# Hybrid encoder layer on eight cores: one halo neighbour per core, first keys from unnormalised x, initial loads in order, halo and memory later

## The reference, cut to what matters

```python
h = rmsnorm(x, norm_gain); proj = h @ w_in          # x: 4 sequences of 4096 rows, D = 2048
q_a,k_a,v_a,z_a, u_b,v_b,z_b, q_c,z_c, gates = split(proj)
# A: |t-s| <= 128 attention, 12 heads over 4 key/value heads of 128, ALiBi, one sink logit
scores = q.k/sqrt(128) - slope*|t-s|;  outside the window or the sequence: -inf
o_a = softmax([scores, sink])[..., :-1] @ v * silu(z_a)
# B: gMLP in chunks of 128 rows: gelu(u) * (w_s[g] @ layernorm(gelu(v)) + b_s[g]) * silu(z_b)
# C: 4 heads of 256 over 256 memory rows: k,v = rmsnorm(mem, mem_norm_gain) @ w_kv_mem
merged = sum over branches of (o @ w_br) * sigmoid(gate)
out = rmsnorm(x + merged @ w_out, final_gain)
```

## Time and profile before

| | us |
|---|---|
| median of 3 runs | 2816.52 |
| lowest, highest | 2794.78, 3295.66 |
| the profiled execution's own time | 2794.82 |
| its span, slowest core (all 8: 2790.7 to 2793.3) | 2793.3 |
| PE busy | 2720.9 |
| DVE, ACT, POOL busy | 869.9, 623.8, 200.6 |

### The profile page before, as it was taken

The page is one execution under the profiler, slowest core; times in us unless marked ns, Lnnn a source line. Parts: engine busy times, 40 slices in busy tenths (PEclk is TensorE's granted clock), DMA queues, the critical chain, the costliest instruction groups (busy, mean ns, idle before and its releaser), DMA issues.

```text
span 2793.3 us, 34510 instructions; the slowest of 8 cores (2790.7 to 2793.3 us)
## 1 busy us (share of the span) xinstructions
PE 2720.9 (97%) x12953; PEld 1280.9 (46%) x13213; DVE 869.9 (31%) x1209; ACT 623.8 (22%) x1183; POOL 200.6 (7%) x381
## 2 busy tenths in 40 slices
PE   5899999999999999999999999999999999999996
PEld 2444456544444444444444444554444444444443
DVE  5600036570641112222450000767063222122224
ACT  3211134434111111111121112543411111111112
POOL 0000000000000000000000000000000000000000
PEclk8999999999999999999999999999999999999998
DMA  9254444624545555444997444222454444444484
GB/s 243 68 91 76 77 82 76 98 53 67 93 84 106 106 106 84 76 76 77 256 221 142 78 77 70 46 46 46 72 88 69 76 76 75 81 78 77 81 196 137
DMA packets 76003, 267.19 MB, mean 96 GB/s; under 512 B 8512, under 2 KB 8640, under 8 KB 74560
## 3 DMA queue, kind: packets, MB, share of 16 engines
q0 software_dynamic: 54288, 197.55, 43.1%
q1 hardware_dynamic: 21552, 67.41, 7.8%
HBM read 445.68 MB, written 16.78 MB: 166 GB/s over the span
## 4 chain that ended last, share of the span: by engine, by line
PE 95%; DVE 3%; issue 1%; ACT 1%; DMA 0%; DVEq 0%; ACTq 0%; SPq 0%
PE ps L333 88%; PE ps L711 2%; PE ps L675 1%; PE ps L678 1%; DVE hT L474 1%; DVE AR L457 1%; PE ps L445 1%; PE ps L772 0%; PE ps L812 0%; DVE OT L1092 0%; PE ps L919 0%; DVE AR L472 0%; DVE AR L474 0%; DMA OT<-xs 0%; DVE GN L726 0%
## 5 line engine op out<-in xcount | busy, mean ns | idle before, releaser
L333 PE MATMUL ps<-hT,RG 128*128 128x512 bf16 x7252 | 1658.7, 380 | 24.0 <-DVE hT L474 12.9
L333 PEld LDWEIGHTS ps<-hT,RG 128*128 128x128 bf16 x7424 | 725.1, 98 | 861.2 <-issue 33.6
L333 PE MATMUL ps<-OT,RG 128*128 128x512 bf16 x2009 | 456.1, 379 | 2.1
L283 POOL DMA_DIRECT2D RG<-wall x376 | 199.9, 532 | 2516.9 <-PE ps L333 1929.1
L726 DVE RECIPROCAL GN<-GN 128x256 f32<-128x256 f32 x96 | 161.5, 1724 | 584.5 <-ACT GN L722 584.5
L958 ACT ACTIVATE GN<-ps 128x512 f32<-128x512 f32 x192 | 113.7, 596 | 882.4 <-PE ps L333 882.4
L333 PEld LDWEIGHTS ps<-OT,RG 128*128 128x128 bf16 x2048 | 200.2, 98 | 240.7
L966 DVE TENSOR_TENSOR GN<-ps,GN 128x512 f32<-128x512 f32 x128 | 88.6, 692 | 550.0 <-PE ps L333 521.5
L333 PE MATMUL ps<-RG,AR 128*128 128x512 bf16 x1050 | 230.7, 379 | 1.2
L333 PE MATMUL ps<-RG,hT 128*128 128x512 bf16 x990 | 221.7, 379 | 1.2
L333 PEld LDWEIGHTS ps<-RG,AR 128*128 128x128 bf16 x1072 | 104.9, 98 | 126.5
(11 more groups left out here) (113 smaller groups left out, 1109.1 us busy)
## 6 DMA issues: line engine op xcount, KB each, us to landing
RG<-wall POOLq DMA_DIRECT2D x376, 512.0 KB, 6.2
OT<-xr SPq DMA_DIRECT2D x16, 1024.0 KB, 17.4
y<-OT SPq DMA_DIRECT2D x32, 512.0 KB, 4.0
OT<-xs SPq DMA_DIRECT2D x8, 1024.0 KB, 19.7
HX<-xr SPq DMA_DIRECT2D x16, 512.0 KB, 6.9
OT<-xt SPq DMA_DIRECT2D x16, 512.0 KB, 20.5
OT<-xh SPq DMA_DIRECT2D x4, 768.0 KB, 16.9
OT<-mt SPq DMA_DIRECT2D x4, 512.0 KB, 8.5
```

Source lines behind the costliest of these rows:

```text
L283: S.op("pool", lambda h: h.dma_start(out=RG[:, sl, :], in_=wall[row * 128:(row + 1) * 128, :]), r=list(gate), w=["R%d" % sl], dma=True)
L333: ins = h.matmul(psb(b, n), lhsT=pairs[i][0], rhs=pairs[i][1], start=(i == 0), stop=(i == N - 1))
```

## The change: what it does

1. **Mirror.** The second half of each sequence is laid out back to front (its rows reversed, the spatial weights and biases reversed with them, and the output turned back). Every core then has the sequence's end on its left and its one neighbour on its right. Block 0 is gone: halo is two blocks (9, 17), 256 rows, and tile 0's first score pack is 256 wide, not 384.
2. **Raw keys.** Slab 0 and slab 1 of x are multiplied by the gain alone into bf16 (`raw_piece`: ACT the first 1 or 2 of four `kc`, DVE the rest), and the key matmuls read that. The factor is applied when the keys leave PSUM (`k_scaled`, DVE). Values and all else still read the normalised `hT`, whose scaling now comes after the first keys.
3. **Loads in order.** x slab 0; key chunk 0 once the third of its four pieces has landed, chunks 1 to 3 behind it; x slab 1 once chunk 2 has landed; chunks 4 to 7 once the third piece of slab 1 has landed.
4. **Halo and memory later.** Their loads follow the first values; sums and scaling are spread over the z stage (`prep`); halo keys and values are computed after it (`kv_halo`), for which the 8 key and value chunks are loaded a second time.
5. Squares are first folded by DVE from four to two (L467), reciprocals come in halves, a table load is taken early, and dummy matmuls (`warm`) stand ahead of and between the first sums. Value evacuations are all ACT's.

```diff
     def tile(first):
         ...
+        if first:
+            p += [("k", g) for g in range(4)] + [("v", 0, q) for q in range(4)]
         for h in range(12):
...
-        HTH_OFF = 20480
-        hTh = view("AR", HTH_OFF, 6144, BF16).rearrange("p (k t) -> p k t", t=384)
+        HTH_OFF = 16384
+        hTh = view("AR", HTH_OFF, 4096, BF16).rearrange("p (k t) -> p k t", t=256)
...
         nS0.load()
-        load_chunk(0)
-        nS1.load()
-        for n in range(1, NSLOT):
-            load_chunk(n, gate=nS0.xc(15))
+        load_chunk(0, gate=nS0.xc(8))
+        for n in range(1, 4):
+            load_chunk(n)
+        nS1.load(gate=["R2"])
+        load_chunk(4, gate=nS1.xc(8))
+        for n in range(5, NSLOT):
+            load_chunk(n)
...
+        warm(48)
+        for p in range(4):
+            nS0.raw_piece(p, 1)
+            nS0.square(p)
+            nS0.fold(p, True)
+            if p < 3:
+                warm(8)
+        nS0.rstd()
...
+        def kv_first():
+            ks = [Ck(0, ("k", g)) for g in range(4)]
...
+            for g in range(4):
+                run(group(kraw(g), 512, "all", k_scaled(g, 1, nS0)))
+            nS0.scale(0, 10)
+            k1 = []
+            for p in range(4):
+                nS1.raw_piece(p, 2)
+                nS1.square(p)
+                nS1.fold(p, False)
+                if p == 0:
+                    k1 = [group(kraw(g), 512, "all", k_scaled(g, 5, nS1)) for g in range(4)]
+                for g in range(4):
+                    if p < 3:
+                        k1[g][p]()
...
+            for g in range(4):
+                k1[g][3]()
...
+            nS0.scale(10, 16)
+            v0 = [v_group(0, v, lb) for lb in range(1, 5)]
+            for q in range(4):
+                for t in range(3):
+                    v0[t][q]()
+                if q == 0:
+                    nS1.total()
+                    nS1.rstd()
+                    for a in hold:
+                        S.op(*a)
+                    nS1.scale()
+            run(v0[3])
+            v1 = [v_group(0, v, lb, sub=1) for lb in range(5, 9)]
+            for kc in range(16):
+                for t in range(4):
+                    v1[t][kc]()
+            v.free()
+            nH.load()
+            nM.load()
...
+                    if tt == 0:
+                        prep({4: 1, 6: 2, 8: 3, 10: 4}.get(ch0 + i, 0))
+            if tt == 0:
+                kv_halo()
```

More of the change, by code:

```diff
@@ new lines, in total, with rstd @@
+            def total(self):
+                w = self.w
+                self.b = bank()
+                S.op("pe", lambda h: h.matmul(psb(self.b, w), lhsT=ONEF[:], rhs=self.ac, start=True, stop=True),
+                     r=["onef"] + self.acc, w=pc(self.b))
+            def rstd(self):
+                w, rs = self.w, self.rs
+                S.op("act", lambda h: h.activation(out=rs, in_=psb(self.b, w), func=AF.Sqrt, scale=1.0 / D,
+                                                   bias=smc(c_eps)), r=["eps"], w=self.rsc + pc(self.b))
+                hw = w // 2
+                for q in range(2):
+                    S.op("dve", lambda h, q=q: h.reciprocal(out=rs[:, q * hw:(q + 1) * hw],
+                                                            in_=rs[:, q * hw:(q + 1) * hw]), w=self.rsc)
@@ L551, in kv_stage, with kv_halo @@
+        def kv_halo():
+            ks = [Ck(0, ("k", g)) for g in range(4)]
+            for g in range(4):
+                c = ks[g]
+                run(group([(c.stat(kc), hTh[:, kc, :], [c.cell] + hthc(kc)) for kc in range(16)], 256, "all",
+                          k_evac(0, g, [9, 17], "dve")))
+                c.free()
+            v = Mv(0, ("v", 0))
+            for lb in (9, 17):
+                run(v_group(0, v, lb))
+            v.free()
         def kv_stage(tt):
+            if tt == 0:
+                kv_first()
+                return
@@ L552, in kv_stage @@
             ks = [Ck(tt, ("k", g)) for g in range(4)]
[L553 to L568, removed]
-                nM.sums()
-            else:
-                for g in range(4):
-                    c = ks[g]
-                    run(group([(c.stat(kc), hT[:, kc, 128:512], [c.cell, hcells(0, kc)]) for kc in range(16)], 384,
-                              "all", k_evac(1, g, [2, 3, 4])))
-                    run(group(hpair(c, 1), 512, "all", k_evac(1, g, [5, 6, 7, 8])))
-                    c.free()
@@ L604, in kv_stage, with prep @@
-            v.free()
+            for g in range(4):
+                c = ks[g]
+                run(group([(c.stat(kc), hT[:, kc, 128:512], [c.cell, hcells(0, kc)]) for kc in range(16)], 384,
+                          "all", k_evac(1, g, [2, 3, 4])))
+                run(group(hpair(c, 1), 512, "all", k_evac(1, g, [5, 6, 7, 8])))
+                c.free()
+            v = Mv(tt, ("v", 0))
+            for lb in range(2, 9):
+                run(v_group(tt, v, lb))
+            v.free()
+        def prep(step):
+            if step == 1:
+                for p in range(4):
+                    nH.square(p)
+                    nH.fold(p, False)
+            elif step == 2:
+                for p in range(4):
+                    nM.square(p)
+                    nM.fold(p, False)
+            elif step == 3:
+                nH.total()
+                nM.total()
+                nH.rstd()
+                nM.rstd()
+                nH.scale()
+                nM.scale()
+            elif step == 4:
+                for k in range(3):
+                    b = bank()
+                    S.op("pe", lambda h, b=b, k=k: h.matmul(
+                        psb(b, 512), lhsT=ONES[:], rhs=WST[:].rearrange("p g t -> p (g t)")[:, k * 512:(k + 1) * 512],
+                        start=True, stop=True), r=["ones", "wst"], w=pc(b))
+                    for gg in range(4):
+                        g = k * 4 + gg
+                        S.op("dve", lambda h, g=g, gg=gg, b=b: h.scalar_tensor_tensor(
+                            out=CC[:, g, :], in0=psb(b, 128, gg * 128), scalar=smc(c_lnb + g), in1=CC[:, g, :],
+                            op0=ALU.mult, op1=ALU.add), r=["lnb"], w=["cc"] + pc(b))
@@ L697, in a_pv @@
                 j = 4 * s + off
+                if tt == 0 and j == 0:
+                    continue
                 qa = max(QB0[j], 4 * s + 1)
@@ L1255 @@
         b, half = c // 2, c % 2
-        out[b, half * 2048:(half + 1) * 2048] = np.asarray(res.results[c]["y"], f32)
+        yc = np.asarray(res.results[c]["y"], f32)
+        out[b, half * 2048:(half + 1) * 2048] = yc if half == 0 else yc[::-1]
     return out
```

264 lines of the change are left out of this document (142 added, 122 removed).

## The result

Over 19 runs each, this kernel's median is 2783.16 us and that of the kernel before 2816.64 us; the ratio is 0.9896, 95% interval [0.9863, 0.993]. Four of these 19 runs and six of the 19 before took over 150 us longer than the rest, in the change with a lower mean granted clock on four or all eight cores, and such runs are left out of the ratio and of all that follows. The kernel is faster by 1.0%, less than the 2% that counts as a difference, and inside the range of 2742 to 2784, but 28 us above the forecast of 2755. In the 15 runs that count the time was one of two: four at 2755.1 to 2755.8, eleven at 2782.0 to 2784.1. For the kernel before, seven of thirteen were at 2794.2 to 2795.1 and six at 2816.5 to 2822.6. So both kernels have an upper and a lower time, and I had forecast the change from lower to lower: 2755.4 / 2794.8 = 0.986.

A forecast was written before the change was run, and what follows sets the result against it. TensorE, busy 97% of the span, was taken as the bound, leaving the first 145 us to gain: start plus halo work 107.8 instead of 145.0 (37.2), attention 2.6, together 39.8 off 2794.8, so 2755; range 2742 to 2784.

The forecast's parts named there:

- Slab 0, first keys: Start of kernel: slab 0's last sums end and key matmuls begin at 24.3 us, 11.5 earlier, done at 38.1.
- The hole: Between first and second keys: TensorE idle 8.4 us while VectorE evacuates, does ten scalings of slab 0, then slab 1's multiplies.
- the half clock: At the start of second keys, after the idleness: first 16 matmuls take 6.9 us instead of 3.45, to 53.4.
- Second keys, values: Second keys end at 63.8 us, values with slab 1's total at 92.3; slab 1 and chunks 4 to 7 land in time.
- Halo later: Halo keys and values after the z stage: 13.8 us of matmuls, near 315 to 329 us, no wait for reloaded chunks.
- The sum: Start and halo work 107.8 us in place of 145.0, gaining 37.2; attention 2.6 more; together 39.8 off 2794.8.
- Transfers late: Rival, chance 0.12: gated transfers queue without overlap, chunk 7 arrives at 81 us, 9 us lost, 2764.
- POOL held while it issues chunks 0 to 3: Variant of late transfers: VectorE's raw multiplies hold POOL up to 2.8 us per issue, chunk 3 some 8 us late.
- ACT as the bound in the z stage: Rival, chance 0.05: squares waiting for the halo's load delay SiLU evacuations, 8.4 us falls on TensorE, 2763.
- The clock staying at half: Rival, chance 0.03: array at 1.2 GHz from first key to last value, kernel slower, 2808.
- Keys that do not start early: Rival, chance 0.02: sums or a late chunk 0 hold keys until 36 us, shifting all by up to 11.5, 2767.

## Why the prediction was right and wrong

**Slab 0, first keys.** Forecast: keys at 24.3, done at 38.1. Measured 24.6 and 38.7. Undoing raw keys moved them to 32.3, undoing the loads to 28.7. (Four key groups are 64 matmuls; the 64 groups of the description of the kernel before are those of its z stage.)

**The hole and the half clock.** Forecast 8.4 us and a charge of 3.45; measured 8.47, and 2.1 by filling it. The charge was too large because the granted clock, 0.50 when second keys began at 47.2, was back at 1.00 from about 51.5, after 4.3 us of work and not 6.9. The raw multiply took 0.87 / 2 = 0.43 where I took 0.50. The estimate that I had worked out from the Trainium skill's figures ("VectorE: DVE Perf Modes", section "The perf-mode tier table") was 0.43, and the trace agrees.

**Second keys, values.** Forecast ends 63.8 and 92.3; measured 63.1 and 91.6. The transfers behind them were less early than forecast, and here some luck was at work. Slab 1 was issued when chunk 2 had landed, at 31.6 on core 3 and at 27.7 to 32.7 over the eight cores, where I had 28.9 for all. Chunks 4 to 7 were issued when its third piece had landed, at 46.3 on core 3 (41.3 to 46.3), where I had 41.9. The hole hid this; the versions that close it ran into it.

**Halo later.** Forecast 315 to 329; measured 314.1 to 328.2, plus a wait of 0.95 us for ACT's last value evacuation that I had not seen. Deferring is worth 20 to 21 us by the experiment.

**The sum.** Forecast 39.8 under the profiled execution. Core 3's span is 2753.2 against 2793.3, 40.1 less. The spans of the cores of one run differ by some 3 us, so that these agree to 0.3 is in part luck; by the lower times of the runs the gain is 2794.8 - 2755.4 = 39.4.

**What failed** is the step from there to the number: "The profiled execution took 2794.8; so 2755". That execution stood at the lower of two times, and the median shown, 2816.5, at the upper. I put the 22 us down to spread between runs, and only in a side sentence said that the middle would then be about 2777. The chances had the same fault: I reckoned the 2% from 2794.8, while against the median shown, 2816.5, my own 2755 was faster by 2.2%. The median came at 2783, 33.5 below the median before where my number stood 61.5 below it. The 22 were not spread: there is nothing between the lower and the upper times (before, four upper times lie 22 us above the lower ones and two 27 to 28; here all eleven lie some 28 above). Here they are seen in the trace of two neighbouring cores at 0.81; in the kernel before no trace has them, and that the cause is the same there is inferred, not shown. The change also has them oftener, 11 of 15 against 6 of 13, which could be chance. From these counts the ratio should be (4 x 2755.4 + 11 x 2783.2) / 15 = 2775.8 over (7 x 2794.8 + 6 x 2818.5) / 13 = 2805.7, so 0.989, as measured. The mechanism of the gain was right; the term missed is the stretch at 0.81, at 28 us a run when it comes. Between the two medians, which are both upper times, the gain is 33.5 us, not 40, since the kernel before mostly lost 22 us and the change 28. Why it loses more stays open. Whether the change brings it on, by reaching full matmul speed at 24 and again at 52 us instead of 48 and 62, stays open.

**The rivals.** Transfers late: hardly in the change (in its profiled run only core 7 waits for a chunk, 0.9 us), but one step away from it, as three experiments show. POOL held while it issues chunks 0 to 3: no, the four issues took 2.41 us on core 3, 0.60 each against 0.53, with VectorE's raw multiplies beside the first of them. ACT as the bound in the z stage: no wait there. The clock staying at half: no, it was full from 51.5 us. Keys that do not start early: no. A third level of the clock was in none of them.

The four parts do not add up: loads 10, raw keys 16, halo later 21, mirror 14, together 61 us for a gain of 40. Each is measured against a kernel that has the others, or none, and what one removes another cannot remove again.

## What to carry to other kernels

Price the start of a kernel as a time line of all engines in their own order: here its main points came out within a microsecond, but look at every core before you call a transfer early. Most of what the change gains comes from taking work off the way to the first matmul and from putting preparation beside work that does not need it. Before subtracting from a profiled execution, look whether the runs shown have more than one time, and say which one the number stands for. Once a hole is closed, the next bound may stand close behind it: here the transfers did, and removing 5.5 us of idle time was worth 2 to 3 us.

## What I had not expected of the hardware

The granted clock was 0.81 on two neighbouring cores from 57 to 216 us and 1.00 on the others. This is seen in one trace. By the spans of the 15 runs of the first comparison, 20 of their 60 pairs of neighbouring cores had lost the same 28 us, and in each run the others stayed near 2753. The Trainium skill, "TensorE: Matmul & The Clock Gate", section "Seeing it yourself", knows a third level of 13/16 = 0.81 that it puts down to a current limit for a whole die of four cores. The level agrees. That it takes the whole die and stays does not fit this trace: a single pair had it and lost it after 159 us, with TensorE as busy as before. In the later sets none of the runs that count had it.
